# GpSimd's modulation sums in fifteen operations of 256 columns in place of five of up to 1024

## What is computed

```
c_act = jax.nn.silu(c)
for l in range(DEPTH):
    mod = c_act @ w_ada[l] + b_ada[l]
    sh1, sc1, gt1, sh2, sc2, gt2 = [m[:, None, :] for m in jnp.split(mod, 6, axis=-1)]
    h = rms_norm(x, norm_mix[l]) * (1.0 + sc1) + sh1
    proj = h @ w_in[l]
    ...
    x = x + gt1 * (merged @ w_o[l])
    h = rms_norm(x, norm_ffn[l]) * (1.0 + sc2) + sh2
    up_act, up_lin = jnp.split(h @ w_up[l], 2, axis=-1)
    ...
    x = x + gt2 * ((jax.nn.silu(up_act) * up_lin) @ w_down[l])
```

## Time and profile before

| | us |
|---|---|
| median of three runs | 2288.85 |
| lowest, highest | 2287.64, 2291.15 |
| profiled execution, whole | 2289.57 |
| profiled execution, its span | 2287.8 |

### The profile page before, as it was taken

The page is one execution under the profiler, slowest core; times in us unless marked ns, Lnnn a source line. Parts: engine busy times, 40 slices in busy tenths (PEclk is TensorE's granted clock), DMA queues, the critical chain, the costliest instruction groups (busy, mean ns, idle before and its releaser), DMA issues.

```text
span 2287.8 us, 39769 instructions
## 1 busy us (share of the span) xinstructions
PE 2183.0 (95%) x17241; PEld 2094.4 (92%) x17241; DVE 1516.7 (66%) x1872; ACT 1075.3 (47%) x1398; POOL 543.1 (24%) x262
## 2 busy tenths in 40 slices
PE   7998999999999989999999999989999999989999
PEld 7987889999989788999999999869999999878999
DVE  6867766677678666667666556776556556686555
ACT  2565464433456546543335335454335334545333
POOL 0871304899348240357000000000000000000000
PEclk7999999999999999999999999999999999989999
DMA  8752245676657304466555555325555556424553
GB/s 285 229 182 69 76 146 184 204 261 235 204 166 224 108 20 157 138 221 211 177 185 178 185 185 169 114 74 185 185 184 167 185 185 183 129 74 148 184 185 128
DMA packets 332855, 383.79 MB, mean 168 GB/s; under 512 B 12551, under 2 KB 315402, under 8 KB 332554
## 3 DMA queue, kind: packets, MB, share of 16 engines
q1 hardware_dynamic: 332234, 381.10, 52.3%
q10 hardware_dynamic: 448, 0.16, 0.0%
HBM read 380.19 MB, written 1.05 MB: 167 GB/s over the span
## 4 chain that ended last, share of the span: by engine, by line
PE 78%; DVE 12%; ACT 7%; issue 3%; DMA 0%; SPq 0%; ACTq 0%; DVEq 0%
PE bank L727 16%; PE bank L728 16%; PE bank L729 16%; DVE weights_low L1348 5%; PE bank L956 5%; PE bank L957 5%; PE bank L958 5%; ACT weights_high L2070 4%; DVE arena L1450 1%; PE bank L741 1%; PE bank L1002 1%; PE bank L1132 1%; PE bank L993 1%; PE bank L1147 1%; PE bank L765 1%
## 5 line engine op out<-in xcount | busy, mean ns | idle before, releaser
L1348 DVE TENSOR_TENSOR weights_low<-ring,weights_high 128x2048 fp32r<-128x2048 f32 x302 | 750.7, 2486 | 440.1 <-ACT weights_high L2070 440.0
L727 PE MATMUL bank<-h_high,weights_high 128*128 128x256 f32 x3296 | 945.7, 287 | 22.3 <-DVE weights_low L1348 13.7
L728 PE MATMUL bank<-h_low,weights_high 128*128 128x256 f32 x3296 | 929.7, 282 | 0.0
L729 PE MATMUL bank<-h_high,weights_low 128*128 128x256 f32 x3296 | 929.1, 282 | 0.0
L2070 ACT ACTIVATE weights_high<-ring 128x2048 fp32r<-128x2048 f32 x302 | 578.0, 1914 | 708.4 <-PE bank L729 546.8
L727 PEld LDWEIGHTS bank<-h_high,weights_high 128*128 128x128 f32 x3296 | 624.2, 189 | 38.6 <-DVE weights_low L1348 21.7
L728 PEld LDWEIGHTS bank<-h_low,weights_high 128*128 128x128 f32 x3296 | 625.3, 190 | 3.4 <-issue 3.3
L729 PEld LDWEIGHTS bank<-h_high,weights_low 128*128 128x128 f32 x3296 | 625.2, 190 | 0.0
L2510 POOL TENSOR_TENSOR side<-side,ccol 128x1024 f32<-128x1024 f32 x80 | 204.2, 2572 | 417.5 <-DVE out_low L1557 139.2
L956 PE MATMUL bank<-hidden_high,weights_high 128*128 128x256 f32 x1056 | 299.8, 284 | 1.5 <-DVE hidden_low L1590 0.8
L957 PE MATMUL bank<-hidden_low,weights_high 128*128 128x256 f32 x1056 | 299.0, 283 | 0.0
(11 more groups left out here) (426 smaller groups left out, 2861.0 us busy)
## 6 DMA issues: line engine op xcount, KB each, us to landing
ring<-in_w_in SPq DMA_DIRECT2D x80, 1024.0 KB, 5.3
ring<-in_w_up SPq DMA_DIRECT2D x44, 1024.0 KB, 5.2
ring<-in_ffn_w_gate SPq DMA_DIRECT2D x44, 1024.0 KB, 5.4
ring<-in_ffn_w_up SPq DMA_DIRECT2D x44, 1024.0 KB, 5.4
ring<-in_ffn_w_down SPq DMA_DIRECT2D x44, 1024.0 KB, 5.0
side<-in_w_ada SPq DMA_DIRECT2D x42, 1024.0 KB, 7.8
ring<-in_w_down SPq DMA_DIRECT2D x22, 1024.0 KB, 5.0
ring<-in_w_dn_out SPq DMA_DIRECT2D x8, 1024.0 KB, 5.2
```

Of the source, the lines that this page charges most:

```text
L727: mm(o[:, m, :], a_, high[:, t, :], start=(t == 0), stop=False)
L728: mm(o[:, m, :], a_, low[:, t, :], start=False, stop=False)
L729: last = mm(o[:, m, :], b_, high[:, t, :], start=False, stop=(t == KT - 1))
L1348: v.tensor_tensor(low, wide(q), high.bitcast(F32), ALU.subtract).then_inc(chunk_split, 1)
```

## The change

Each of the first three levels of `side_sum` is written as operations on one block of 256 columns: eight multiplications in place of two of 1024 columns, four additions in place of one of 1024, two in place of one of 512. The last addition was of 256 columns already and stays. The waits between the levels are as they were, one after each level; the same elements are multiplied and added in the same pairs. `side_sum` is called forty times, so GpSimd gets 400 instructions more. The instructions of the other engines and their order are the same.

```
-                then(*[g_.tensor_tensor(w[:, u:u + 4, :], w[:, u:u + 4, :], bcast(ccol[:, u:u + 4], 256), ALU.mult) for u in (0, 4)])
-                then(g_.tensor_tensor(w[:, 0:4, :], w[:, 0:4, :], w[:, 4:8, :], ALU.add))
-                then(g_.tensor_tensor(w[:, 0:2, :], w[:, 0:2, :], w[:, 2:4, :], ALU.add))
+                then(*[g_.tensor_tensor(w[:, u:u + 1, :], w[:, u:u + 1, :], bcast(ccol[:, u:u + 1], 256), ALU.mult) for u in range(KT)])
+                then(*[g_.tensor_tensor(w[:, u:u + 1, :], w[:, u:u + 1, :], w[:, u + 4:u + 5, :], ALU.add) for u in range(4)])
+                then(*[g_.tensor_tensor(w[:, u:u + 1, :], w[:, u:u + 1, :], w[:, u + 2:u + 3, :], ALU.add) for u in range(2)])
                 c0 = 256 * (SIDE[j][1] % 4)
                 g_.tensor_tensor(acc[:, n % 2, c0:c0 + 256], w[:, 0, :], w[:, 1, :], ALU.add).then_inc(side_summed, 1)
```

## The result

| | before | after |
|---|---|---|
| median, us | 2289.7 | 2309.3 |
| lowest, highest, us | 2287.6, 2291.2 | 2307.7, 2311.4 |
| profiled execution, span, us | 2287.8 | 2309.1 |
| TensorE's mean granted clock | 0.978 | 0.974 |

The ratio is 1.0085, with a 95% interval of 1.0073 to 1.0098. The change costs 19.7 us. The forecast was 2291.1, and its range ended at 2301: the result lies outside, at the height of the worst price of the first rival, though that price was not paid for its reason.

What follows compares the result with a forecast made beforehand. TensorE, busy 95%, bounds the kernel; GpSimd's time counts only where someone waits for it. Terms 4.4 + 2.0 - 0.4 - 3.8 = +2.2 us on the median of 2288.9 give 2291.1 us; range 2283 to 2301.

Steps and rivals of the forecast that it cites:

- the worst price of the first rival: GpSimd's sums: each 256-column multiplication at 0.73 us, +2.4 us a sum, +18.6 us in all, 2308 us.
- the first rival: GpSimd's sums outrun the ring: dearer operations, a sum of about 10.0 us or more, 2300 to 2308 us; chance 0.31.
- the two ends of `w_o`: Both layers, ahead of `modc`: two longer sums move L993 by 2.2 us each time, together +4.4 us.
- the squares of `kd`: Layer 0, L2492 behind four longer sums: TensorE waits about 0.9 us, +2.0 us in all; nothing in layer 1.
- the ffn of layer 0: Late loads of pieces and chunks cost TensorE 5.0 us, shorter waits behind VectorE give 5.4: net -0.4 us.
- all the rest: Ffn of layer 1 and four single waits elsewhere: shorter operations give TensorE 1.8 + 2.2, with 0.2 left, -3.8 us.
- The cost of a sum alone: GpSimd's sum without contention: 9.7 us in place of 8.30, 1.4 us more for each of forty sums.
- VectorE's waits at most 0.7 us: VectorE's L1348 beside GpSimd's shorter operations would wait 0.7 us at most, which TensorE would not notice.
- TensorE's waits for `weights_low` below 8 us in all: Sign that the forecast is right: these TensorE waits, 15.8 us before, fall below 8 us over the span.
- the three places: Where idle time doesn't hide longer sums: end of `w_o` +4.4 us, squares of `kd` +2.0, ffn of layer 0 net -0.4.
- The second and third: Rivals on GpSimd's queue: fixed part hides in it, 2281 us, chance 0.14; GpSimd keeps its turn, 2315 us, chance 0.05.
- Its rule of 1.2 us for each 0.1 us of sum: First rival: the three places together lose some 1.2 us for each 0.1 us that a sum costs more.

Runs made afterwards that it cites:

- coarse_more_work: The kernel before with one more 512-column addition in each sum, whose result nobody reads: 2302.3 us, ratio 1.0058.
- fine_less_work: The changed kernel with only two of the four first-level additions made, so a sum alone is as long as before: 2269.4 us, ratio 0.9916.
- coarse_spread: The kernel before with the twelve loads of pieces in the ffn of layer 0 spread over 32 chunks, not 28: 2284.4 us, ratio 0.9983.

## Why the prediction was wrong, step by step

**The sum, as it came out.** By the table of starts the two ends of `w_o` cost 4.5 us (4.4 forecast), the squares of `kd` 13.6 (2.0), the ffn of layer 0 10.1 (-0.4), and all the rest gave 7.7 (3.8): +20.6 in place of +2.2. The step that failed is the time of a sum beside VectorE. The forecast let a sum grow by the 1.4 us that it grows alone, with one L1348 more in four sums at most. Ahead of the squares four sums grew by 10.6 and 8.5 us, in the ffn each of nine by 2.5. The second step that failed is the spare time at the squares of `kd`: TensorE came there earlier in layer 0, and in layer 1 another reader's spare time was read.

**The cost of a sum alone: right.** 9.7 us forecast, 9.72 measured, each level within 0.1. The estimate from the Trainium skill (GPSIMD Engine Reference, Performance pitfalls for Q7 kernels) was 1.7 us more for a sum; the trace has 1.42. VectorE's waits at most 0.7 us: right, 0.48 in the ffn of layer 0 and 0.64 anywhere. TensorE's waits for `weights_low` below 8 us in all: wrong, 19.6, since the late chunks are in them.

**The end of w_o: right.** L993 was to move by 2.2 us in each layer. TensorE waits 2.75 us for the sum, and the stretch from the 39th to the 43rd chunk grows by 2.3 us, that of layer 1 by 2.2.

```profile
424.39 0.83 PE L993 MATMUL bank<-constants,acc 128*128 128x1 f32 x6 [2.75 <-POOL acc L2514]
```

**The squares of kd: mis-sized, 2.0 forecast against 7.6 in layer 0 and 6.0 in layer 1.** L2492 ends in layer 0 at 148.3, where the forecast had 147.9, but that is luck. The sums began 2.5 us earlier than before, at 76.31 in place of 78.82. From there to L2492 they took 70.9 us in place of 60.3, 10.6 more and not 7.65, since two L1348 more fall into them and not one. The two errors nearly cancel. TensorE comes there 3.9 us earlier, at 143.2. Its wait at 65 us is 1.1 us shorter, with no stretch at half speed behind it, and that at 139 is 1.5 us shorter. The forecast had credited 1.0 us of this and left TensorE's arrival at 147.07. So TensorE waits 5.1 us and not 0.9, and its clock stands at half speed for 6.8 us from 146.2 on.

```profile
148.32 1.22 PE L815 MATMUL bank<-gbb,constants 128*128 128x512 f32 x1 [5.14 <-POOL gbb L2492]
```

In layer 1 the forecast put nothing, because of 5.46 us of idle time ahead of L2534. That idle time lies behind L2492. What TensorE can spare at L815 is the time from the end of L2492, 729.98, to its own arrival, 738.07: 8.1 us. The four sums and the squares among them run from 681.88 to 750.61, 68.7 us, where the kernel before needs from 668.68 to 728.94, 60.3. That is 8.5 us more, with one L1348 more in them, and L2492 itself stands behind a second:

```profile
750.61 3.09 POOL L2492 TENSOR_TENSOR gbb<-kd 128x512 f32<-128x512 f32 x1
```

Together it ends 10.5 us later in relation to the start of the sums, TensorE comes 1.6 us earlier, and it waits 4.1 us.

**The ffn of layer 0: mis-sized, -0.4 forecast against +10.1.** Four sums were to end 5.6 to 6.6 us later than before in relation to the ffn's start; they ended 8.3 later (494.67 - 433.94 = 60.7 in place of 52.5), and the last piece went out 18.1 later. There the load of before had stopped waiting for its sum, and the sum itself was 24.2 late. The fourth piece, which the forecast looked at in full, cost 2.5 us of TensorE's waits and not 3.8. The others, which it had in a clause at 1.2, cost 2.9, 1.2, 1.9 and 3.2: 11.7 in all, where the kernel before waits 5.4. From the 43rd chunk to the 76th TensorE's idle time grows by 6.4 us (from 215.9 - 207.11 to 226.03 - 210.83), and its matmuls take 3.7 us longer; the two make up the 10.1.

What the forecast left out is that a longer sum takes in more of VectorE's work. An L1348 comes each 6 us and takes some 2.05 us from GpSimd, a third of the time. So 1.42 us alone become 1.42 / (1 - 0.34) = 2.2, an estimate, and 2.5 were measured. coarse_more_work has 2.0 for 1.35.

**The gain: taken too low.** Outside the three places I gave 3.8 us to shorter waits; by the table it was 7.7, and at the old length of a sum short operations gave 19.5. The forecast counted TensorE's waits and left out what some of them do to the clock.

**The missing term: the clock.** Half-speed stretches grow by 17 us between 55 and 1250 us, and over the whole span the same matmuls take 5.4 us longer. TensorE's idle time between 55 and 1250 us grows from 59.7 to 75.6 us. Not every such stretch can be put down to the change: one also appears or goes where nothing else differs (in layer 1 behind the first stage, 1.7 us in several of the runs).

**The rivals.** The first had the right mechanism, sums that outrun the ring, but it was tied to dearer operations, which did not come. It should have been tied to the time of a sum as it runs beside VectorE. Its rule of 1.2 us for each 0.1 us of sum is near what long operations show (13.4 us for 1.35, 1.0 for each 0.1), and far from what short ones do (39.2 us between fine_less_work and the changed kernel for 1.38, 2.8 for each 0.1). The second and third did not occur: a queued operation of 256 columns overlaps the next by 0.04 us, and L1348 never waits for a run of operations.

## What to carry to other kernels

A helper engine that shares a resource with another should be costed by the time its work takes beside the other, not alone: each added microsecond takes in more of the other's instructions, here 2.5 us in all for 1.4. Take the spare time of a reader at the reader, not at the next idle time of the helper. List each reader of such work with its spare time, follow a lag that accumulates to its last reader, and when a gain brings the reader earlier, take it off its spare time. Where long operations block and short ones cost, try the size between: half the length cost 0.4 us a sum and won 13 to 16 us; a quarter cost 1.4 and lost 20.

## What the runs showed of the hardware that was not expected

A GpSimd operation of two different tensors costs 0.18 us and 2.13 ns a column, one with a broadcast column 0.18 us and 1.67 ns; queued ones overlap by 0.04 us. That holds for 256, 512 and 1024 columns. VectorE gets its turn even in a run of eight queued operations of 0.6 us: of 26 L1348, none waited more than 0.48 us.

Each L1348, 2.29 us alone, takes about 2.0 us from GpSimd. In single rows that is 2.07 and 2.06 for the multiplications of 1024 and 256 columns, 1.98 and 2.10 for the first additions. Why the additions differ was not tried.

Many of TensorE's longer waits are followed by 3.4 or 6.8 us at half speed: in the changed kernel those of 2.9, 2.5, 1.9 and 3.2 us in the ffn of layer 0, in the one before that of 1.5 us at 534. Not all are: those of 2.4 us at 139, 2.2 at 178 and 1.5 at 267 in the kernel before were not, nor that of 1.2 us at 552 in the changed one, and in coarse_spread the same wait of 2.4 us at 139 was. No wait of 0.2 to 0.8 us in the ffn of layer 0 was. One stretch at half speed, from 626.4 to 630.0 us in the kernel before, has no wait of TensorE over 0.15 us in the 48 us ahead of it. So a long wait can cost more than its length, but its length alone doesn't tell whether it does, and the runs don't show what decides.
